# A two-model transformer kernel: the rounded weights of two of the last three down pieces of each first-model network go to slots of their own, and three pieces of the stage behind are rounded ahead of the last down products

## The reference, cut to what matters

```python
def first_block(x, ...):
    x = layer_norm(x, ln_in_g, ln_in_b)
    for l in range(DEPTH):                       # DEPTH = 2
        proj = jnp.einsum('bsd,de->bse', x, w_in[l])
        ...
        x = layer_norm(DN_ALPHA * x + mix, ln1_g[l], ln1_b[l])
        gu = jnp.einsum('bsd,df->bsf', x, w_ffn_in[l])
        hidden = jax.nn.silu(gu[..., :D_FF]) * gu[..., D_FF:]      # D_FF = 2816
        ffn = jnp.einsum('bsf,fd->bsd', hidden, w_ffn_out[l])
        x = layer_norm(DN_ALPHA * x + ffn, ln2_g[l], ln2_b[l])
    return x

def second_block(x, ...):
    for i in range(DEPTH):
        h = rms_norm_2(x, attn_norm_g[i])
        proj = h @ w_in[i]
        ...
```

## Time and profile before

| | |
|---|---|
| median of three runs | 1450.3 us (1450.12 to 1450.74) |
| the profiled execution: its own time | 1450.26 us |
| span of its trace, first to last instruction | 1449.0 us |
| PE busy | 1435.8 us (99%) |
| DVE busy | 1040.4 us (72%) |
| ACT busy | 812.9 us (56%) |
| mean rate of the DMAs | 180 GB/s |
| granted TensorE clock | 1.000 |

### The profile page before, as it was taken

The page is one execution under the profiler, slowest core; times in us unless marked ns, Lnnn a source line. Parts: engine busy times, 40 slices in busy tenths (PEclk is TensorE's granted clock), DMA queues, the critical chain, the costliest instruction groups (busy, mean ns, idle before and its releaser), DMA issues.

```text
span 1449.0 us, 19722 instructions
## 1 busy us (share of the span) xinstructions
PE 1435.8 (99%) x7721; PEld 1210.3 (84%) x7721; DVE 1040.4 (72%) x1423; ACT 812.9 (56%) x1177; POOL 60.9 (4%) x100
## 2 busy tenths in 40 slices
PE   8999999999999999999999999999999999999999
PEld 7888878888887888887888888788888888888888
DVE  6766976755557566875865556877988868788886
ACT  6565554454543565754454444676655657775563
POOL 1000000000001000000100000210000012000000
PEclk9999999999999999999999999999999999999999
DMA  8754635566665464642756565436556644456651
GB/s 272 249 191 148 227 122 174 176 203 188 200 210 190 154 214 122 218 145 93 253 183 221 184 199 174 146 109 211 174 189 200 217 131 163 142 178 202 196 184 58
DMA packets 172684, 261.09 MB, mean 180 GB/s; under 512 B 9520, under 2 KB 111568, under 8 KB 172336
## 3 DMA queue, kind: packets, MB, share of 16 engines
q1 hardware_dynamic: 171296, 255.18, 53.7%
q0 software_dynamic: 1152, 4.65, 1.0%
q10 hardware_dynamic: 144, 0.01, 0.0%
HBM read 256.66 MB, written 1.05 MB: 178 GB/s over the span
## 4 chain that ended last, share of the span: by engine, by line
PE 94%; DVE 4%; POOL 1%; ACT 0%; DMA 0%; issue 0%; SPq 0%; DVEq 0%; ACTq 0%
PE ps L458 16%; PE ps L534 12%; PE ps L536 12%; PE ps L535 12%; PE ps L459 9%; PE ps L428 7%; PE ps L432 6%; PE ps L430 6%; PE ps L461 2%; PE ps L486 1%; PE ps L835 1%; PE ps L1077 1%; DVE wlo L1715 1%; PE ps L638 1%; DVE x L1774 1%; DVE x L1772 1%
## 5 line engine op out<-in xcount | busy, mean ns | idle before, releaser
L1715 DVE TENSOR_TENSOR wlo<-raw,whi 128x2048 fp32r<-128x2048 f32 (+1 forms) x234 | 519.5, 2229 | 228.2 <-ACT whi L1193 228.2
L1193 ACT ACTIVATE whi<-raw 128x2048 fp32r<-128x2048 f32 (+1 forms) x234 | 434.6, 1867 | 139.1 <-PE ps L536 52.2
L458 PE MATMUL ps<-xT,whi 128*128 128x512 f32 x1008 | 356.5, 396 | 0.0
L459 PE MATMUL ps<-xT,wlo 128*128 128x256 f32 x1152 | 311.6, 281 | 0.0
L534 PE MATMUL ps<-whi,xT 128*128 128x512 f32 (+3 forms) x640 | 250.4, 391 | 1.6 <-DVE xT L1793 1.2
L536 PE MATMUL ps<-whi,xT 128*128 128x512 f32 (+3 forms) x640 | 242.3, 379 | 0.0
L535 PE MATMUL ps<-wlo,xT 128*128 128x512 f32 (+3 forms) x640 | 241.6, 377 | 0.0
L458 PEld LDWEIGHTS ps<-xT,whi 128*128 128x128 f32 x1008 | 189.4, 188 | 41.9
L459 PEld LDWEIGHTS ps<-xT,wlo 128*128 128x128 f32 x1152 | 217.6, 189 | 6.1
L534 PEld LDWEIGHTS ps<-whi,xT 128*128 128x128 f32 x640 | 120.5, 188 | 23.7 <-issue 4.4
L536 PEld LDWEIGHTS ps<-whi,xT 128*128 128x128 f32 x640 | 120.3, 188 | 22.5
(11 more groups left out here) (244 smaller groups left out, 1964.3 us busy)
## 6 DMA issues: line engine op xcount, KB each, us to landing
raw<-in_w_in SPq DMA_DIRECT2D x120, 512.0 KB, 4.7
raw<-in_w_ffn_in SPq DMA_DIRECT2D x88, 512.0 KB, 4.8
raw<-in_w_up SPq DMA_DIRECT2D x88, 512.0 KB, 4.8
raw<-in_w_ffn_out SPq DMA_DIRECT2D x44, 512.0 KB, 4.3
raw<-in_w_down SPq DMA_DIRECT2D x44, 512.0 KB, 4.3
raw<-in_w_branch SPq DMA_DIRECT2D x24, 512.0 KB, 4.8
raw<-in_w_out SPq DMA_DIRECT2D x16, 512.0 KB, 4.1
raw<-in_w_o SPq DMA_DIRECT2D x16, 512.0 KB, 4.5
```

The source lines that it names most:

```text
L458: PE.matmul(ps[:, b, :], hi, m.xT[:, kt], start=kt == 0, stop=False)
L459: mm = PE.matmul(ps[:, b, 0:S], lo, m.xTh[:, kt], start=False, stop=False)
L1193: AC.activation(m.whi[:, i % SPLIT, 0:w], m.raw[:, slot, 0:w], ACT.Copy).then_inc(s.w_hi, 1)
L1715: DV.tensor_tensor(m.wlo[:, i % SPLIT, 0:w], m.raw[:, slot, 0:w], m.whi[:, i % SPLIT, 0:w].bitcast(F32), ALU.subtract).then_inc(s.w_lo, 1)
```

## The change

- Two more slots for rounded halves. D8 goes to slot 4, D9 to slot 5 (`rounding_slots`, `weights_of`); their halves lie in `proj` and `gate`. All other pieces go round the four slots without counting D8 and D9, and each waits for the last user of its own slot.
- `aside(c, held)` moves the calls of `split_to` in steps 9 and 10 on ACT and DVE: two pieces more are rounded ahead from there on.
- `split_to(later + 3)` stands ahead of the last `add_down`s on both engines, where it was `later + 2` on ACT and `later + 1` on DVE.
- The rotation tables of the second model move from `gate` to the idle part of `rpb` (`m.tables`).

```diff
+def aside(c, held):
+
+    return (c > NSTEP - 3) * min(held + (c == NSTEP - 1), 2)
+
+def rounding_slots(pieces, first):
+
+    aside = {first[1, L, "dn", NSTEP - 3 + i]: SPLIT + i for L in range(DEPTH) for i in range(2)}
+    slots, last, turn = [], {}, 0
+    for i in range(pieces):
+        slot = aside.get(i, turn % SPLIT)
+        turn += i not in aside
+        slots.append((slot, last.get(slot)))
+        last[slot] = i
+    return slots
+
+def weights_of(k, i):
+
+    slot = k.slots[i][0]
+    if slot < SPLIT:
+        return k.m.whi[:, slot], k.m.wlo[:, slot]
+    return tuple(x[:] for x in k.m.more[slot - SPLIT])
...
+        homes = [at["proj"] + 4 * (2 * PROJ - (i + 1) * PIECE) for i in range(3)] + [at["gate"]]
+        aside = [nc.alloc_sbuf_tensor_at(f"aside{i}", [P, PIECE], F32R, offset=o) for i, o in enumerate(homes)]
...
@@ scalar_program, split_to
-            if i >= SPLIT:
-                AC.wait_ge(s.w_used, i - SPLIT + 1)
-            AC.activation(m.whi[:, i % SPLIT, 0:w], m.raw[:, slot, 0:w], ACT.Copy).then_inc(s.w_hi, 1)
+            if k.slots[i][1] is not None:
+                AC.wait_ge(s.w_used, k.slots[i][1] + 1)
+            AC.activation(weights_of(k, i)[0][:, 0:w], m.raw[:, slot, 0:w], ACT.Copy).then_inc(s.w_hi, 1)
@@ scalar_program, steps 2 to 10 of the network
             low_out(c, 0)
             gate_silu()
-            split_to(k.after[up] - 1 + SPLIT)
+            split_to(k.after[up] - 1 + SPLIT + aside(c, 1))
             low_out(c, 1)
             if c < NSTEP - 1:
-                split_to(k.after[up] + SPLIT)
+                split_to(k.after[up] + SPLIT + aside(c, 1))
             features_hi(c)
             if c < NSTEP - 1:
-                split_to(k.after[1, L, "dn", c - 2] + SPLIT)
+                split_to(k.after[1, L, "dn", c - 2] + SPLIT + aside(c, 2))
         later = k.after[1, L, "dn", NSTEP - 1]
-        split_to(later + 2)
+        split_to(later + 3)
@@ vector_program, the same steps
             features_out(c, 0)
-            split_to(k.after[up] - 1 + SPLIT)
+            split_to(k.after[up] - 1 + SPLIT + aside(c, 1))
             features_out(c, 1)
             features_gated()
             if c < NSTEP - 1:
-                split_to(k.after[up] + SPLIT)
+                split_to(k.after[up] + SPLIT + aside(c, 1))
             features_lo(c)
             if c < NSTEP - 1:
-                split_to(k.after[1, L, "dn", c - 2] + SPLIT)
+                split_to(k.after[1, L, "dn", c - 2] + SPLIT + aside(c, 2))
         later = k.after[1, L, "dn", NSTEP - 1]
-        split_to(later + 1)
+        split_to(later + 3)
         add_down(0, (1, L, "dn", NSTEP - 1))
```

More of the change, by code:

```diff
@@ L70 @@
 Sems = namedtuple("Sems", SEMS)
-Tensors = namedtuple("Tensors", [n for n, _, _ in SBUF] + ["ps", "down", "cw", "sgw", "brow", "xTh", "xTl"])
-Kernel = namedtuple("Kernel", "nc t out m s raws leads free size first after call bank halves seen")
+Tensors = namedtuple("Tensors", [n for n, _, _ in SBUF] + ["ps", "down", "cw", "sgw", "brow", "xTh", "xTl", "tables", "more"])
+Kernel = namedtuple("Kernel", "nc t out m s raws leads free size first after call bank halves seen slots")
 class Count(defaultdict):
@@ L145, in build @@
     with ExitStack() as ctx:
-        sb = [ctx.enter_context(nc.sbuf_tensor(name, shape, dt)) for name, shape, dt in SBUF]
+        sb, at = [], {}
+        for name, shape, dt in SBUF:
+            at[name] = nc.sbuf_base
+            sb.append(ctx.enter_context(nc.sbuf_tensor(name, shape, dt)))
+        homes = [at["proj"] + 4 * (2 * PROJ - (i + 1) * PIECE) for i in range(3)] + [at["gate"]]
+        aside = [nc.alloc_sbuf_tensor_at(f"aside{i}", [P, PIECE], F32R, offset=o) for i, o in enumerate(homes)]
         ps = ctx.enter_context(nc.psum_tensor("ps", [P, 8, 512], F32))
@@ L356, in rope_tables @@
                     angle = m.rope[:, th, 48 + 32 * j:80 + 32 * j].rearrange("p (a d) -> p a d", a=2)
-                    c0 = D + 768 + i * 128 + j * 64
-                    o = PO.tensor_tensor(m.gate[:, th, c0:c0 + 64].rearrange("p (a z d) -> p a z d", a=2, z=2),
+                    c0 = i * 128 + j * 64
+                    o = PO.tensor_tensor(m.tables[:, th, c0:c0 + 64].rearrange("p (a z d) -> p a z d", a=2, z=2),
                                          spread(angle, [P, 2, 2, 16], 2), gain, ALU.mult)
@@ L410, in gemm @@
             w = c * width * len(outs(0))
-            views.append([x[:, (i0 + i) % SPLIT, 0:w].rearrange("p (k n w) -> p k n w", k=c, w=width)
-                          for x in (m.whi, m.wlo)])
+            views.append([x[:, 0:w].rearrange("p (k n w) -> p k n w", k=c, w=width) for x in weights_of(k, i0 + i)])
         for th in ths:
@@ L444, in by_features @@
             for kt in range(8):
-                slot, j, end = (i0 + kt // 4) % SPLIT, kt % 4, kt == 7
+                i, j, end = i0 + kt // 4, kt % 4, kt == 7
                 before(pair, kt)
@@ L450, in by_features @@
                     o, b = j * 2 * FC + f * P, f ^ first
-                    hi, lo = [x[:, slot, o:o + P] for x in (m.whi, m.wlo)]
+                    hi, lo = [x[:, o:o + P] for x in weights_of(k, i)]
                     if not joined:
@@ L522, in half @@
         for i, count in enumerate(kts):
-            hi, lo = [x[:, (i0 + i) % SPLIT, 0:count * width].rearrange("p (k w) -> p k w", k=count)
-                      for x in (m.whi, m.wlo)]
+            hi, lo = [x[:, 0:count * width].rearrange("p (k w) -> p k w", k=count) for x in weights_of(k, i0 + i)]
             if th == 0:
@@ L1152, in last_down @@
             i = k.first[2, L, "dn", c]
-            hi, lo = [x[:, i % SPLIT, :].rearrange("p (k n w) -> p k n w", k=2, n=2) for x in (m.whi, m.wlo)]
+            hi, lo = [x.rearrange("p (k n w) -> p k n w", k=2, n=2) for x in weights_of(k, i)]
             for b, o in enumerate(narrow(1)):
@@ L1714, in split_to @@
             DV.wait_ge(s.w_hi, i)
-            DV.tensor_tensor(m.wlo[:, i % SPLIT, 0:w], m.raw[:, slot, 0:w], m.whi[:, i % SPLIT, 0:w].bitcast(F32),
+            hi, lo = weights_of(k, i)
+            DV.tensor_tensor(lo[:, 0:w], m.raw[:, slot, 0:w], hi[:, 0:w].bitcast(F32),
                              ALU.subtract).then_inc(s.w_lo, 1)
@@ L2270, in rotate_rows @@
             w = m.gate[:, th, c0:c0 + 64 * heads].rearrange("p (h e) -> p h e", e=64)
-            cos, sin = [m.gate[:, th, D + 768 + i * 128 + j * 64:D + 832 + i * 128 + j * 64] for j in range(2)]
+            cos, sin = [m.tables[:, th, i * 128 + j * 64:i * 128 + j * 64 + 64] for j in range(2)]
             DV.tensor_tensor(w, x, spread(sin, [P, heads, 64]), ALU.mult)
```

5 lines of the change are left out of this document (3 added, 2 removed).

## The result

Five runs of the changed kernel gave 1455.25 to 1459.32 us, median 1458.57; five of the kernel before, 1450.12 to 1451.10, median 1450.39. The ratio is 1.0052, 95% interval 1.0041 to 1.0063. The forecast was 1455.1 us with a range of 1451.0 to 1457.5: the direction was right, the size was not. The profiled execution took 1459.32 us, with a span of 1458.0 us and a granted clock of 0.996. In the five runs clock and time go together: 0.996 for 1458.57, 1458.78 and 1459.32 us, 0.998 for 1457.64, 0.999 for 1455.25. The runs of the kernel before that stood beside the experiments all had 1.000.

What follows compares the result with a forecast made beforehand. PE was taken to bound the kernel from end to end, with gaps at the two boundaries. Losses of 3.1 and 1.7 us, gains already in them, made 4.8 us over 1450.3: 1455.1 us, range 1451.0 to 1457.5.

Steps and rivals of the forecast that it cites:

- N0's landing: Load queue: N0 lands at 437.0 behind the parameters despite earlier issue, while its upper half stands ahead of `low_out(10, 0)`, due 435.28.
- The second rival: N0's landing follows its issue, 1.85 us earlier at each boundary: 1451.4 us, chance 0.10.
- The chain to D10: From N0's landing through ACT and DVE to the hidden features: 449.5 against 446.10, so PE stands 3.4 us.
- The gains: Two lower halves taken off DVE behind the boundaries: 0.7 us at the first, 2.1 at the second, together 2.8 us.
- the sum: Losses of 3.1 us at the first boundary and 1.7 at the second, 4.8 us more than 1450.3: 1455.1 us.
- first rival: N0 lands by about 433.6, features are ready for PE, the gain comes whole: 1447.5 us, chance 0.08.
- Nothing: tables and slots: Tables in `rpb` instead of `gate`, other addresses for two pieces, same instruction and DMA counts: no cost.
- Moved: D8, D9 and D10, at nothing: Step 9: D8 and D9 each push ACT by 1.9 and DVE by 2.2 us, under cover of step 10's products: no cost.
- the cost of the stand: PE's 3.4 us wait ahead of D10 at each boundary, priced in the time lost with no loss of clock.
- third rival: Stall also costs clock: D10's first 12 products at half rate, 2.7 us per boundary less 0.4; 1459.7 us, chance 0.08.
- my case: N0 lands late, PE stands 3.4 us ahead of D10 at each boundary, 1455.1 us; chance 0.70.
- the bounds of the landing: N0's landing: at best 1.85 us earlier at each boundary, 3.7 us off; at worst 0.5 us later each, 1 us more.

Runs made afterwards that it cites:

- filled one: The changed kernel with 14 unread products on PE between D9 and D10 of the first half: 1455.26 us, ratio 1.0033.
- Without the stand: The changed kernel with the norm's two parameter DMAs issued behind N2 instead of between D10 and N0: 1448.30 us, ratio 0.9986.
- the last kernel: The changed kernel with parameters behind N2, transposes of x's second half earlier, and DVE's lower half of N0 behind the first sum: 1446.14 us, ratio 0.9971.

## Why the prediction had the wait right and the time wrong

- **The deciding term, N0's landing, was right.** On the old scale 437.25 against 437.0, and an earlier issue did not help. SP issues N0 in the changed kernel at 428.51, 0.8 us earlier than in the earlier trace rows, or 1.4 on the old scale, and its two DMAs take that much longer: 8.3 us in the mean instead of the 6.8 of the earlier trace rows. With the parameters out of the way they take 5.2. The second rival (the landing follows the issue) is out. The Trainium skill's rule (DMA: Bandwidth & Descriptors, section Queues, rings and completion order) is that each engine takes the descriptors of one ring in order. The landings agree with it: N0 at 437.25 behind the parameters, and with the parameters issued behind it, its upper half at 433.65. No trace here shows the order within one engine.
- **The chain to D10 was right.** PE stood 3.46 and 3.51 us, forecast 3.4. `add_down(0)` was forecast to wait for DVE alone; at the first boundary it waited 1.07 us for PE in the changed kernel, and not for PE in the filled one, so that wait belongs to the clock.
- **The gains were there, in part.** The filled kernel's 1455.26 us are within 0.2 us of the sum, with errors of about 0.5 us in its two parts that cancel. Without the stand the gains gave 1448.3 us (first rival: 1447.5). From the trace before to that one, less what it is early ahead of each boundary, they are 0.1 us at the first (470.92 against 471.24) and 1.5 at the second (916.04 against 917.74), where the forecast had 0.7 and 2.1. The first rival asked only that D10 be in time, and left out that N2's lower half then makes `add_down(0)` late: 0.7 us at the first boundary. With N0's lower half moved behind the first sum this is gone too.
- **"Nothing: tables and slots": right**, by the run with the slots alone. **"Moved: D8, D9 and D10, at nothing": right**, by the last kernel, which has these moves, no wait for D10 and `add_down(0)` at its old time.
- **The term that was mis-sized is the cost of the stand.** The sum priced it at its own length, with the clock unchanged; I put the loss of clock aside as the third rival, with a chance of 0.08. It is no rival to my case: it comes on top of it, in all five runs to some extent (clock 0.996 to 0.999) and in four of them by enough to leave the forecast by 2.5 us and more. Measured as changed kernel against filled one, it is 1458.57 - 1455.26 = **3.3 us**. The rival had 4.6, with 2.3 at each boundary; the rows give 1.33 at the first, where only some seven products ran at half rate, and 2.26 at the second, where all 12 did. In the text stood what should have moved the chance: behind 6.4 us of idle time four transposes had taken 1.12 us instead of 0.66, behind 1.1 us the rate had stayed, and 3.4 lay between. That is a case with no row for it, nearer to even chances than to 0.08. (The evidence of the start is weaker than it looked: the granted clock of the window 7 to 8 us reads 1.00 there, although the transposes are slow.) The Trainium skill (TensorE: Matmul & The Clock Gate, the part on the HAM clock gate) has the clock fall from 2.4 to 1.2 GHz when TensorE has been idle. The trace of the changed kernel agrees: 0.92 and 0.70 in windows in which PE did nothing.
- **The range** took in the bounds of the landing and the second rival but left out the third, on the side where the result fell.

What stays open is which stands lose the clock. Waits of 1.7 us and 1.96 us did not in the profiled executions, one of 2.32 did, and so did 2.63, 3.46 and 3.51; in some other runs of the same kernels the mean clock was 0.999 or 1.000. These rows don't tell what else decides.

## What to carry to other kernels

Before a piece of work is moved ahead of a short copy on the critical chain, ask what is ahead of its data on the DMA queue, not when it is issued: here two parameter loads of 512 KB, whose data the norm takes 20 us later, decided between 8 us lost and 2 us won. When a forecast lets TensorE stand for about 2 us or more in a kernel that otherwise hardly pauses (here 1.96 us kept the clock and 2.32 lost it), price the products behind the stand at half rate in the same sum, not as a separate case. A small loss that varies from run to run together with the granted clock is a sign of such a stand; filling it with idle products separates the wait from the clock in one run.

## What the runs showed of the hardware that was not expected

- The granted clock fell around stands of TensorE as short as 2.32 us: in the stand itself in the changed kernel (0.92 and 0.70 in windows without a product), and behind the one of 2.32 us only when D10 was running again (1.00 from 900 to 901, 0.85 from 901 to 902). It does not cost the same each time: the five runs of the changed kernel spread over 4.1 us (1455.25 to 1459.32), those of the filled one over 1.0 us.
- How long the half rate lasts behind like stands differs: some seven products behind 3.46 us, all 12 behind 3.51 us, in one execution.
- 28 products that nobody reads made the kernel 3.3 us faster.
- Two 512 KB loads that copy one row of 4 KB to 128 partitions, ahead in the queue, set the landing of those behind them: N0's two DMAs took 8.3 us behind them and 5.2 us without them. Behind N0 on the queue, they did not delay it (433.65 against 433.76).
